# Query projections of a split-precision transformer block: one 512-column and one 256-column product, or three of 256 columns

## What is computed

```
h    = modulate(rms_norm(x,   norm1_g), sh1, sc1)      # 256 latent tokens
hc   = modulate(rms_norm(ctx, norm1_g), csh1, csc1)    # 256 context tokens
qa, ka, va, qb, kb, vb = split_projection(h @ w_in[:, :6144])
_,  ka_c, va_c, _, kb_c, vb_c                          = split_projection(hc @ w_in[:, :6144])
a_lat = neighbourhood_attention(qa, ka, va, ka_c, va_c, rpb)          # 8 heads of 128
b_lat = diff_attention(rope(qb), rope(kb), vb, kb_c, vb_c, lam)       # 8 heads of 2 x 64
x = x + g1 * merge_branches(a_lat, b_lat, gates, ...)
x = x + g2 * conv_ffn(modulate(rms_norm(x, norm2_g), sh2, sc2), ...)
out = rms_norm(x, final_norm_g)
```

## Time and profile before

| | |
|---|---|
| median of 3 runs | 1719.82 us (1719.37 to 1722.01) |
| profiled execution, its own time | 1720.02 us |
| its span | 1718.3 us |
| TensorE matmuls busy | 1677.8 us (98%), 8768 instructions |
| TensorE weight loads busy | 1371.5 us (80%), 8768 instructions |
| VectorE busy | 1086.3 us (63%) |
| ScalarE busy | 752.6 us (44%) |
| GpSimd busy | 108.6 us (6%) |
| mean DMA rate | 216 GB/s |

### The profile page before, as it was taken

One profiled execution on the slowest core, in us unless ns is written; L12 is line 12 of the kernel. 1 busy time (PEld: TensorE's weight loads), 2 busy tenths in 40 slices (PEclk: granted clock), 3 DMA queues, 4 the chain that ended last, 5 costly groups with the idle time before them and its releaser, 6 DMA issues.

```text
span 1718.3 us, 23725 instructions
## 1 busy us (share of the span) xinstructions
PE 1677.8 (98%) x8768; PEld 1371.5 (80%) x8768; DVE 1086.3 (63%) x1366; ACT 752.6 (44%) x962; POOL 108.6 (6%) x161
## 2 busy tenths in 40 slices
PE   4999999999999999999999999999999999999997
PEld 1568888888888678888888788888888888888886
DVE  1338787768887674554555666666666666655556
ACT  2233321623222664444444555555555555544444
POOL 0002222122121000000000000000000000000000
PEclk7999999999999999999999999999999999999999
DMA  9999888269896128566565566666666665655552
GB/s 353 386 387 347 298 296 297 79 215 328 259 321 200 52 90 271 191 189 191 192 234 195 148 190 190 188 191 188 191 187 191 185 184 188 202 195 194 191 193 83
DMA packets 161813, 371.47 MB, mean 216 GB/s; under 512 B 11671, under 2 KB 12423, under 8 KB 160598
## 3 DMA queue, kind: packets, MB, share of 16 engines
q1 hardware_dynamic: 140240, 291.65, 52.5%
q0 software_dynamic: 20144, 74.22, 12.7%
q10 hardware_dynamic: 1366, 4.74, 0.7%
HBM read 368.36 MB, written 2.21 MB: 216 GB/s over the span
## 4 chain that ended last, share of the span: by engine, by line
PE 94%; DMA 3%; DVE 1%; issue 0%; ACT 0%; SPq 0%; DVEq 0%; POOL 0%; ACTq 0%
PE ps L1885 21%; PE ps L1884 11%; PE ps L1899 10%; PE ps L1901 10%; PE ps L1900 10%; PE ps L2253 5%; PE ps L2252 5%; PE ps L2254 5%; PE ps L1811 4%; PE ps L1813 3%; PE ps L1812 3%; DMA raw<-in_ada_w 3%; PE ps L1882 1%; PE ps L1803 1%; PE ps L1968 1%; PE ps L1950 1%
## 5 line engine op out<-in xcount | busy, mean ns | idle before, releaser
L1147 DVE TENSOR_TENSOR w_lo<-raw,w_hi 128x1024 fp32r<-128x1024 f32 x480 | 584.5, 1223 | 419.7 <-ACT w_hi L680 419.2
L680 ACT CAST w_hi<-raw 128x1024 fp32r<-128x1024 f32 x480 | 503.4, 1050 | 763.3 <-PE ps L1885 271.2
L1885 PE MATMUL ps<-h2T,w_hi 128*128 128x512 f32 x1320 | 462.7, 394 | 0.0
L1884 PE MATMUL ps<-h2T,w_lo 128*128 128x256 f32 x1320 | 366.8, 278 | 0.0
L1885 PEld LDWEIGHTS ps<-h2T,w_hi 128*128 128x128 f32 x1320 | 247.8, 188 | 53.7
L1884 PEld LDWEIGHTS ps<-h2T,w_lo 128*128 128x128 f32 x1320 | 248.2, 188 | 3.9
L1899 PE MATMUL ps<-w_hi,hT 128*128 128x512 f32 x512 | 201.7, 394 | 0.0
L1901 PE MATMUL ps<-w_hi,hT 128*128 128x512 f32 x512 | 199.4, 389 | 0.0
L1900 PE MATMUL ps<-w_lo,hT 128*128 128x512 f32 x512 | 199.3, 389 | 0.0
L1222 DVE SCALAR_TENSOR_TENSOR ada_acc<-ada_raw,silu_c,ada_acc 128x512 f32<-128x512 f32 x240 | 179.9, 750 | 29.4 <-DMA ada_raw<-in_ada_w 14.1
L603 POOL DMA_DIRECT2D ada_raw<-in_ada_w x128 | 91.2, 712 | 381.5 <-DVE ada_acc L1222 226.4
(11 more groups left out here) (231 smaller groups left out, 1985.6 us busy)
## 6 DMA issues: line engine op xcount, KB each, us to landing
raw<-in_ffn_w_up SPq DMA_DIRECT2D x176, 512.0 KB, 3.8
raw<-in_w_in SPq DMA_DIRECT2D x152, 512.0 KB, 4.8
ada_raw<-in_ada_w POOLq DMA_DIRECT2D x128, 512.0 KB, 5.9
raw<-in_ffn_w_down SPq DMA_DIRECT2D x88, 512.0 KB, 4.3
raw<-in_ada_w SPq DMA_DIRECT2D x64, 512.0 KB, 10.4
raw<-in_w_out SPq DMA_DIRECT2D x32, 512.0 KB, 4.4
raw<-in_w_branch_a SPq DMA_DIRECT2D x16, 512.0 KB, 3.6
raw<-in_w_branch_b SPq DMA_DIRECT2D x16, 512.0 KB, 3.6
```

The source lines that it names most:

```text
L680: act.copy(w_hi[:, s % SPLIT_SLOTS, :], raw[:, s, :]).then_inc(hi_ready[s], 1)
L1147: dve.tensor_tensor(w_lo[:, s % SPLIT_SLOTS, :], raw[:, s, :], w_hi[:, s % SPLIT_SLOTS, :], ALU.subtract).then_inc(lo_ready[s], 1)
L1884: pe.matmul(ps[:, b + t, 0:SEQ], w_lo[:, row4(s), at], high(kc), start=False, stop=False)
L1885: return pe.matmul(o, w_hi[:, row4(s), at], both(kc), start=False, stop=(kc == KC - 1))
```

## The change

The query jobs get a function of their own, `unit_q`. It issues three matmuls of 256 moving columns for each `kc` and tile: `w_hi` by the high part, `w_hi` by the low part, `w_lo` by the high part, all three added into the same 256 columns. Two output tiles share a bank, so a job fills banks `b` and `b + 1` and leaves `b + 2` and `b + 3` alone. Only the first matmul of the even tile in a bank carries `start`. ScalarE reads the two banks whole, 128 x 1024 elements as before, and counts `q_read` itself. VectorE's `read_result` and its two calls are gone, and so is the semaphore `half_read`. Nothing else is changed.

```diff
-                elif j < JOB_DIFF:
-                    act.copy(qT[:, TILES * g:TILES * (g + 1), :], ps[:, b:b + 4, 0:SEQ]).then_inc(half_read, 1)
                 else:
-                    act.mul(qT[:, TILES * g:TILES * (g + 1), :], ps[:, b:b + 4, 0:SEQ], DIFF_SCALE)\
-                        .then_inc(half_read, 1)
+                    heads = qT[:, TILES * g:TILES * (g + 1), :].rearrange("p (a t) n -> p a (t n)", a=2)
+                    if j < JOB_DIFF:
+                        act.copy(heads, ps[:, b:b + 2, :]).then_inc(q_read, 1)
+                    else:
+                        act.mul(heads, ps[:, b:b + 2, :], DIFF_SCALE).then_inc(q_read, 1)
...
-            def read_result(j):
-                kind, col = PROJECTIONS[j - JOB_NA]
-                if kind != "q":
-                    return
-                g = (col // GROUP) % 2
-                b = 4 * (j % 2)
-                q = qT[:, TILES * g:TILES * (g + 1), :]
-                dve.wait_ge(half_read, g + 1 + (2 if j >= JOB_DIFF else 0))
-                if j < JOB_DIFF:
-                    dve.tensor_tensor(q, q, ps[:, b:b + 4, SEQ:2 * SEQ], ALU.add).then_inc(q_read, 1)
-                else:
-                    dve.scalar_tensor_tensor(q, ps[:, b:b + 4, SEQ:2 * SEQ], DIFF_SCALE, q, ALU.mult, ALU.add)\
-                        .then_inc(q_read, 1)
...
-                    if s == 3:
-                        read_result(j - 1)
...
-                    if s == 3 and j > JOB_DIFF:
-                        read_result(j - 1)
...
+            def unit_q(s, t, b):
+
+                o = ps[:, b + t // 2, t % 2 * SEQ:(t % 2 + 1) * SEQ]
+                for i in range(2):
+                    kc = 2 * s + i
+                    at = slice(i * GROUP + t * P, i * GROUP + (t + 1) * P)
+                    hi, lo = w_hi[:, row4(s), at], w_lo[:, row4(s), at]
+                    pe.matmul(o, hi, hT[:, 0, 0, kc, :], start=(kc == 0 and t % 2 == 0), stop=False)
+                    pe.matmul(o, hi, hT[:, 0, 1, kc, :], start=False, stop=False)
+                    mm = pe.matmul(o, lo, hT[:, 0, 0, kc, :], start=False, stop=(kc == KC - 1 and t % 2 == 1))
+                return mm
...
-                            mm = unit_paired(s, t, b, lambda kc: hT[:, 0, :, kc, :], lambda kc: hT[:, 0, 0, kc, :])
+                            mm = unit_q(s, t, b)
```

More of the change, by code:

```diff
@@ L379, in block_program @@
         mod_ready = sem("mod_ready")
-        half_read = sem("half_read")
         kv_read = sem("kv_read")
```

## The result

The changed kernel takes 1723.16 us (median of 20 runs, 1721.25 to 1725.58), the kernel before 1719.93 us (median of 20, 1718.24 to 1722.01). The ratio is 1.0019, with a 95% interval of 1.0013 to 1.0025: slower by 3.2 us, between 2.2 and 4.3 us. The point forecast was 1724.0, the fixed price alone gave 1723.4.

The account below looks back on a forecast made before the run. TensorE was taken to bound the kernel. From the profiled 1720.0 us, +3.4 for added matmuls, +0.65 for short behind short and zero for the readers gave 1724.1, stated as 1724.0; range 1717.5 to 1726.5 us.

Parts of the forecast that it names:

- What bounds the kernel: Whole kernel: TensorE, busy 98% of the span; its time changes in query jobs reach the end one for one.
- Part 1, the fixed price: Query jobs: each matmul with its load costs 13.3 ns besides its columns; 256 added ones make +3.4 us.
- Part 2, short behind short: Query jobs: a 256 following a 256 costs up to 1.7 ns extra at 768 places; half taken, +0.65 us.
- Bounds of parts 1 and 2: Query jobs: from -5.0 us (weight loads at the transposes' 109 ns) to +7.3 us (18.3 ns over each 256's columns).
- The Trainium skill's 2.5 ns: Query jobs: published gap of N / 2.4 ns plus 2.5 per isolated matmul, making the change cost 0.6 us.
- Part 3, the readers: VectorE and ScalarE in query jobs: losing four additions, 4.9 us in all, is covered by TensorE; ScalarE's read unchanged; zero.
- A: Rival for query jobs: 13.3 ns per matmul and load over its columns; 1723.4 to 1724.8 us, chance 0.52.
- B: Rival for query jobs: a 256 takes what its starts say, 117 ns; three take 350 ns, +0.9 us; chance 0.24.
- C: Rival for query jobs: price proportional to columns, a 256 takes 113.3 ns, -1.7 us; loads alone, 1715.0 us; chance 0.09.
- D: Rival for query jobs: instruction supply limits short matmuls to 127 ns each, three take 380 ns, +8.5 us; chance 0.15.
- the line of 0.2%: Whole kernel: about 0.2% (3.4 us) is what a measurement can tell from no change.
- the even split between slower and same: Whole kernel: chances of 0.50 for slower by over 0.2%, 0.46 for the same, 0.04 for faster.

Follow-up runs that it names:

- split-only: Kernel before with three 256-column products per pair in the query jobs, old places in four banks, both readers kept: 1723.08 us, ratio 1.0019.
- split up-projection: Kernel before with 1408 up-projection pairs made into three products of 256 columns each, query jobs unchanged: 1739.09 us, ratio 1.0108.

## Why the prediction was right

**What bounds the kernel**: right. TensorE is busy for the whole of each query job in both profiles, the one group of long waits is the same, and the 3.25 us between the start of query job 1 and L2125, of 3.4 asked for, are the growth of the four query jobs.

**Part 1, the fixed price**: right, to the accuracy of the trace. 120 ns a start were forecast for a 256 among 256s and 120 were read, 359.8 ns for three. The argument (one constant explains 226.7 and 346.7 ns) held for the third size, the 256 alone, that the two sums contain. As a law it fails on both sides: under full loads the pace doesn't fall below 111.6 ns, so 128 columns don't take 66.7; and with half a load a 512 doesn't get cheaper.

**Part 2, short behind short**: wrong in its size and its place, +0.65 us where there was none. The step that failed is to charge slot 0's excess to the place: "in the new code a 256 always follows a 256; before, that is so only in slot 0". The excess of slot 0 is there (697 against 693.3 ns in a long run, twice the 1.7 ns read from four groups), but in an unbroken run of 256s there is none; what slot 0 has and the new code has not is long and short in one run. With the upper bound of 1.3 us the sum would be +4.7 us, outside the measured 2.2 to 4.3. Without this term the forecast is 1723.4, nearer to 1723.16.

**Bounds of parts 1 and 2**: the lower one took the transposes' 109 ns for the pace of loads; with fp32r weights 111.6 was read. Whether the 109 are the loads' at all is open. The attention scores of the kernel before multiply plain fp32 operands, as the transposes do, and their four products of 256 columns

```profile
330.64 1.03 PE L1917 MATMUL ps<-kT,qT 128*128 128x256 f32 x4
```

stand some 216 ns apart, about what twice their columns take at 2.4 GHz (213.3); 109 ns is in the same way near twice 128 columns (106.7).

The Trainium skill's 2.5 ns ("TensorE: Matmul & The Clock Gate", section "Back-to-back issue gap") speaks of an isolated matmul. The measurement disagrees with it here: its 0.6 us lies below the interval, and 256 columns took 120 ns, not 109.2.

**Part 3, the readers**: right, and tested alone: 1.0001 without the additions. `q_read` comes 7 us earlier than before, not 6 (162.1 + 1.2 against 155.3 + 1.0), on which nothing rests. ScalarE's read was taken as unchanged, and its record in the changed kernel says so:

```profile
L777 ACT COPY qT<-ps x2: 1009/1009/1009, 157.0 to 225.3; 128x1024 f32<-128x1024 f32 x2
```

**The rivals**: A came out. B rested on the starts of two 256s between 512s (117 ns each), and those starts were true. In the 39 pairs of the earlier trace rows too the next start comes 115 ns after a 256 and 231 ns after a 512, on average; only the sum of the two is 346.7. So in a mixed run the distance behind a matmul is not that matmul's own price, and B was right that the missing part shows at the 512s. Its error was to take the short distance with it into a run without 512s: the split-only and the changed kernel both begin a query job with two short distances, then settle at 0.12 us. C fell with the first 120 ns. D fell in the split up-projection: 360 ns for three over the whole stage.

**The range and the chances**: 1723.16 lies in the range. The effect landed on the line of 0.2% (0.19%), as the working said it might, so the even split between slower and same was all that the rows could give.

## What to carry to other kernels

Where TensorE is never idle, count matmuls as well as columns: at the upper clock an fp32r matmul of 512 or 256 columns with a full weight load costs 13.3 ns over its columns in a long run of its kind, so one of 512 beats two of 256 by that much, and pieces of 192 and of 128 columns stood 111.6 and 111.7 ns apart, hardly closer than the 120 ns of a 256. Work taken off an engine that has slack pays for none of it. A constant that explained two sums held for the size that both contain and failed below it, at 192 and 128 columns. And a pace belongs to a long run of one kind: read it from such a run, not from the two or three matmuls at a boundary.

## What was not expected of the hardware

- Products with full 128-column fp32r loads keep 111.6 to 111.7 ns, whether 128 or 192 columns are streamed; the step from there to 120 ns at 256 columns isn't a limit of the load.
- Half the stationary columns take a 256 from 120.0 to 113.3 ns, and a 512 from 226.7 to 229.8. The second is unexplained.
- Blocks of 512s and 256s in one run cost more than the same matmuls in alternation: 697 against 693.3 ns for four, 1402.9 against 1386.7 for eight. Also unexplained. Alternation, as the kernel before has it, is the best of the three orders that were run.
- At the lower clock the 13.3 ns are gone. In the profiled execution of the kernel before, pairs at a granted clock of 0.50 stand 0.64 us apart, which is 768 columns at 1.2 GHz (640 ns) with nothing over:

```profile
978.42 0.63 PE L1882 MATMUL ps<-h2T,w_hi 128*128 128x512 f32 x1
...
979.06 0.63 PE L1882 MATMUL ps<-h2T,w_hi 128*128 128x512 f32 x1
```

No version here beats the kernel before. The ones that ran below it (192 columns, half the stationary columns) leave out part of the sums.
